# A longer lead in the gather stages of a two-layer decoder step: picks two rounds and values four rounds behind the spread

## The reference

```python
def peer(h, w_q, sub_k1, sub_k2, u_tab, v_tab):
    ...
        v1, i1 = lax.top_k(s1, P_TOPK)
        v2, i2 = lax.top_k(s2, P_TOPK)
        ...
        eid = jnp.take_along_axis(cid, j, axis=-1)
        g = jax.nn.softmax(sc.astype(F32), axis=-1)
        act = jax.nn.gelu(jnp.einsum('td,thkd->thk', xc, u_tab[eid]).astype(F32))
        return jnp.einsum('thk,thkd->td', g * act, v_tab[eid].astype(F32)).astype(h.dtype)
```

## Time and profile before

| | |
|---|---|
| runs | 2349.54, 2355.18, 2357.84 us, median 2355.18 |
| span of the profiled execution | 2353.7 us, first to last instruction |
| PE | 2044.5 us busy, 87% of the span |
| PEld | 1496.2 us, 64% |
| DVE | 1177.2 us, 50% |
| POOL | 1001.2 us, 43% |
| ACT | 650.0 us, 28% |
| gathers (software DMA queue) | 310.68 MB, 36.3% of what 16 DMA engines could be busy |
| mean granted clock of PE | 0.934 of 2.4 GHz |

### The profile page before, as it was taken

One profiled execution on the slowest core, in us unless ns is written; L12 is line 12 of the kernel. 1 busy time (PEld: TensorE's weight loads), 2 busy tenths in 40 slices (PEclk: granted clock), 3 DMA queues, 4 the chain that ended last, 5 costly groups with the idle time before them and its releaser, 6 DMA issues.

```text
span 2353.7 us, 38380 instructions
## 1 busy us (share of the span) xinstructions
PE 2044.5 (87%) x14289; PEld 1496.2 (64%) x14289; DVE 1177.2 (50%) x3447; ACT 650.0 (28%) x977; POOL 1001.2 (43%) x874
## 2 busy tenths in 40 slices
PE   9889999999997667889898889999999986777777
PEld 4554899999995323334356346999999973233332
DVE  2554699423333533578456834997233333333333
ACT  1332244545551001112134022454555520000000
POOL 0111469830004565656514303688500026666665
PEclk9899999999998798999997989999999998888878
DMA  6473434444447999999932334244444469999998
GB/s 233 173 279 119 144 129 159 161 162 162 168 163 264 331 355 369 362 329 335 350 122 62 90 116 152 81 161 153 162 168 164 165 217 348 360 346 357 365 357 312
DMA packets 179914, 529.91 MB, mean 225 GB/s; under 512 B 22066, under 2 KB 49234, under 8 KB 179474
## 3 DMA queue, kind: packets, MB, share of 16 engines
q0 software_dynamic: 87296, 310.68, 36.3%
q1 hardware_dynamic: 91282, 216.25, 26.8%
q10 hardware_dynamic: 1152, 0.52, 0.1%
HBM read 524.69 MB, written 2.69 MB: 224 GB/s over the span
## 4 chain that ended last, share of the span: by engine, by line
PE 68%; another core or an unknown queue 8%; DVE 8%; POOL 5%; issue 5%; DMA 3%; ACT 2%; SPq 1%; DVEq 0%; ACTq 0%; PEldq 0%
PE bank L950 10%; PE bank L952 10%; PE bank L951 10%; PE bank L769 8%; PE bank L1014 8%; PE bank L990 4%; POOL u_low L703 3%; PE bank L1032 3%; PE bank L1092 2%; DVE i_one_hot L2172 2%; DMA v_slot<-in_peer_v,v_rows 2%; POOL v_slot L712 2%; PE bank L979 1%; PE bank L1242 1%
## 5 line engine op out<-in xcount | busy, mean ns | idle before, releaser
L712 POOL DMA_INDIRECT v_slot<-in_peer_v,v_rows x417 | 394.6, 946 | 703.8 <-PE bank L952 441.1
L950 PE MATMUL bank<-h_parts,u_high 128*128 128x288 f32 x2048 | 607.0, 296 | 7.9 <-POOL u_low L703 6.2
L951 PE MATMUL bank<-h_parts,u_high 128*128 128x288 f32 x2048 | 604.4, 295 | 0.0
L952 PE MATMUL bank<-h_parts,u_low 128*128 128x288 f32 x2048 | 602.8, 294 | 0.0
L950 PEld LDWEIGHTS bank<-h_parts,u_high 128*128 128x128 f32 x2048 | 384.1, 188 | 11.6 <-POOL u_low L703 9.6
L952 PEld LDWEIGHTS bank<-h_parts,u_low 128*128 128x128 f32 x2048 | 385.8, 188 | 0.0
L951 PEld LDWEIGHTS bank<-h_parts,u_high 128*128 128x128 f32 x2048 | 384.6, 188 | 0.0
L1597 ACT CAST u_high<-u_slot 128x1024 fp32r<-128x1024 f32 x256 | 268.7, 1050 | 400.5 <-PE bank L952 249.1
L703 POOL TENSOR_TENSOR u_low<-u_slot,u_high 128x1024 fp32r<-128x1024 f32 x120 | 321.1, 2686 | 93.5 <-ACT u_high L1597 93.4
L1014 PE MATMUL bank<-v_slot,weight_columns 128*32 128x512 f32 x1412 | 274.1, 687 | 57.3 <-DMA v_slot<-in_peer_v,v_rows 34.1
L1014 PE MATMUL bank<-v_slot_of_columns,weight_columns 128*32 128x512 f32 x636 | 246.2, 687 | 69.8 <-DVE weight_columns L2179 44.0
(11 more groups left out here) (393 smaller groups left out, 2463.2 us busy)
## 6 DMA issues: line engine op xcount, KB each, us to landing
u_slot<-in_peer_ut SPq DMA_DIRECT2D x256, 512.0 KB, 3.5
w_q<-in_peer_w_q SPq DMA_DIRECT2D x8, 2048.0 KB, 14.4
region<-in_cache_a_kt SPq DMA_DIRECT2D x8, 960.0 KB, 11.8
region<-in_cache_a_v SPq DMA_DIRECT2D x8, 960.0 KB, 11.4
v_slot<-in_peer_v,v_rows POOLq DMA_INDIRECT x417
region<-in_ev_w_in SPq DMA_DIRECT2D x3, 2048.0 KB, 15.1
region<-in_pool_kv POOLq DMA_DIRECT2D x40, 128.0 KB, 5.0
ckv_t_norm<-in_pool_ckv SPq DMA_DIRECT2D x64, 64.0 KB
```

Source lines behind the costliest of these rows:

```text
L712: pool.indirect_dma_start(out=VS[l][slot], out_offset=None, in_=v_rows, in_offset=bass.IndirectOffsetOnAxis(ap=IDX[:, at:at + 1], axis=0)) ...
L950: pe.matmul(bank, uh, HR[:, 0, c, :], start=(c == 0), stop=False)
L951: pe.matmul(bank, uh, HR[:, 1, c, :], start=False, stop=False)
L952: ins = pe.matmul(bank, ul, HR[:, 0, c, :], start=False, stop=(c == KC - 1))
```

## The change

Two constants set the lead: the pick runs two rounds behind the spread, the values four. PE's round r does the spread of group r, the pick of group r-2 and the values of group r-4, over 76 rounds. DVE's iteration q does first the weights of group q-2, then the one-hot of group q. The waits and signals move from the helpers to the place of the call, and each step has its own wait in front of it. The wait of the one-hot for the pick of q-2 is gone as a line of its own, since the weights of q-2, which come before it on DVE now, wait for the same. The places of the key projections move back by one round (the first twenty) and by two (the others), the S5 doublings by two iterations, and the four single increments of `key_squares_used` become one of four on the last matmul. In the first layer DVE's norm of the next layer moves behind the loop, and the last tile's sum with it. Two strings of the slot plan are renamed.

```diff
+PICK_LAG, VALUE_LAG = 2, 4
+ROUNDS = NGR + VALUE_LAG
...
-NORM_PLACES = ([(q, third) for q in range(29, 39) for third in (0, 1)]
-               + [(q, third) for q in range(43, 72) for third in (0, 1, 2) if third < 2 or q % 3 == 1][0:60])
+NORM_PLACES = ([(q, third) for q in range(30, 40) for third in (0, 1)]
+               + [(q, third) for q in range(45, 74) for third in (0, 1, 2) if third < 2 or q % 3 == 1][0:60])
...
                     for i in range(4):
-                        pe.matmul(banks[7 if k else 5][32 * i:32 * i + 32, :], SUMW[:, m, :], KSQ[k // 2][:, i, :], start=(m == 0), stop=(m == 3),
-                                  skip_group_check=True).then_inc(sem("key_squares_used"), 1)
+                        ins = pe.matmul(banks[7 if k else 5][32 * i:32 * i + 32, :], SUMW[:, m, :], KSQ[k // 2][:, i, :], start=(m == 0), stop=(m == 3),
+                                        skip_group_check=True)
+                    ins.then_inc(sem("key_squares_used"), 4)
...
-                for q in range(NGR + 2):
-                    if q < NGR:
-                        spread_i1(q)
-                    key_norms(q, 0)
-                    if 1 <= q <= NGR:
-                        pick(q - 1)
-                    key_norms(q, 1)
-                    if l == 0 and q == NGR + 1:
+                for r in range(ROUNDS):
+                    if r < NGR:
+                        if r >= 2:
+
+                            pe.wait_ge(sem("one_hot_ready"), NGR * l + r - 1)
+                        spread_i1(r).then_inc(sem("i1_spread"), 1)
+                    key_norms(r, 0)
+                    if PICK_LAG <= r < NGR + PICK_LAG:
+                        pe.wait_ge(sem("one_hot_ready"), NGR * l + r - PICK_LAG + 1)
+                        if r >= PICK_LAG + 2:
+
+                            pe.wait_ge(sem("weights_ready"), NGR * l + r - PICK_LAG - 1)
+                        pick(r - PICK_LAG).then_inc(sem("picked_full"), 1)
+                    key_norms(r, 1)
+                    if l == 0 and r == ROUNDS - 1:
 
                         pe.wait_ge(sem("weights_ready"), NGR)
                         odd_norm(0)
                         odd_norm(1)
-                    if q >= 2:
-                        values(q - 2)
-                    key_norms(q, 2)
+                    if r >= VALUE_LAG:
+                        pe.wait_ge(sem("weights_ready"), NGR * l + r - VALUE_LAG + 1)
+                        values(r - VALUE_LAG).then_inc(sem("v_used"), 1)
+                    key_norms(r, 2)
...
-                for q in range(NGR + 2):
+                for q in range(NGR + PICK_LAG):
+                    if q >= PICK_LAG:
+                        weights(q - PICK_LAG)
                     if q < NGR:
+                        dve.wait_ge(sem("i1_spread"), NGR * l + q + 1)
                         one_hot(q)
-                    if 1 <= q <= NGR:
-                        weights(q - 1)
-                    if l == 0 and q == NGR + 1:
-                        odd_var(0)
-                        odd_var(1)
-                        odd_scale(0)
-                        odd_scale(1)
-                        odd_turned(0)
-                        odd_turned(1)
-                    if q - 2 in lasts:
-                        add_tile(lasts[q - 2], q - 2)
+                    if q - VALUE_LAG in lasts:
+                        dve.wait_ge(sem("v_used"), NGR * l + q - VALUE_LAG + 1)
+                        add_tile(lasts[q - VALUE_LAG])
...
-                        n = q - (first + 32)
+                        n = q - (first + 34)
...
+                if l == 0:
+                    odd_var(0)
+                    odd_var(1)
+                    odd_scale(0)
+                    odd_scale(1)
+                    odd_turned(0)
+                    odd_turned(1)
+                dve.wait_ge(sem("v_used"), NGR * (l + 1))
+                add_tile(1)
```

48 lines of the change are left out of this document (19 added, 29 removed).

## The result

The changed kernel takes 2366.39 us (median of six runs), the kernel before 2355.34 us beside it. The ratio is 1.0057, with an interval of 1.0039 to 1.0074: the change is 0.57% slower, where 0.57% faster was forecast, and the time lies outside the range. The profiled execution spans 2364.8 us, 11.1 us more than that of before.

What follows compares the result with a forecast made beforehand. Prediction: DMA engines bound the two gather stages, in the second layer held back by PE waiting for DVE's weights. 10.5 + 4.3 + 1.0 + 1.5 - 3.9 = 13.4 us off the 2353.7 span, plus 1.5 to the median: 2341.8 us, range 2330 to 2360.

Steps and rivals of the forecast that it cites:

- PE can follow: 259.90 us busy for 59 groups, 4.4 us a group: Second layer: PE needs 4.4 us a group, against 5.91 now, so PE keeps up with faster gathers.
- The stall goes to the landing of the gather: Second layer: PE's 46.3 us wait for weights goes; PE waits for gathers instead, 60 us or more, up from 21.
- The second layer, 10.5 us: Second layer's gathers: 350 us at 355 GB/s become 339.5 at 366, 10.5 us gained, bounds nothing and 27.
- The ceiling of 366 GB/s: Gather stages: rate divided by DMA share is 363 to 368 GB/s; 366 taken for an always busy DMA with gathers alone.
- The first layer, 4.3 + 1.0 + 1.5 us: Gains in the first layer's gathers: 4.3 at 980 to 1120 us, 1.0 at 1120 to 1170, 1.5 during S5 factors.
- The start, 3.9 us for both: Start of each gather stage: values of group 0 come 1.9 us later, 3.9 us lost in both layers, upper bound 12.5.
- Signals and places, 0: Moved waits, increments, key projections and S5 turns: 0 taken; projections and turns at most 2 us either way.
- at most 1 us gained: End of first layer: DVE's final work moves behind the loop, W_in1 loads wait for unchanged group 70; 0 taken.
- slower by PE's clock: Rival, second layer: granted clock falls below 0.76 and PE bounds, 2370 us; 0.10 shared with a start at its upper bound.
- The ceiling (2355): Rival, gather stages: DMA already at its ceiling, second layer gains 0 to 3 us, first 2, starts cost 3.9; chance 0.27.
- The rival for a start at its upper bound: Stage starts: two whole rounds of 3.1 us lost a layer, above 2359 us; 0.10 shared with the slower clock.
- if POOL still resumes late because the signal of a used slot is itself late, which the lead does nothing about: Sign of being wrong, gather stages: POOL's wait for used slots stays late despite the lead; no size given.

Runs made afterwards that it cites:

- free gathers: Changed kernel; values multiply rows of X, a gather into a used slot waits only for the landing before it: 2720 us, on the second kind of chip 2244.2.
- plain loads: Kernel with values on X, but SP loads rows in order in the second layer, up to eight in flight: 2241.8 us (second kind), 5.17 us a group (first).
- short start: Changed kernel; each stage's first four rounds keep lead one and two, rounds 4 and 5 carry no values: 0.9998 of before (first kind), 0.31% and 0.43% faster (second).

## Why the prediction was wrong

**What bounded the kernel.** Right: DVE's weights were what PE named, and the wait went. Wrong: that the gathers' rate is held by this wait. The step that failed is "PE can follow: 259.90 us busy for 59 groups, 4.4 us a group": it took PE's pace as its own, while on this kind of chip it is 12.9 instructions a us with three gathers in flight and 5.3 with four, and one every 1.40 us under free gathers. "The stall goes to the landing of the gather" failed with it. It went into stops of PE, 29.3 to 54.6 us, and into matmuls that take longer in the record (271 us busy for 340 us at a clock of 0.99, against 260 for 350 at 0.85). That PE falls behind under gathers is shown by the free gathers and by the plain loads on the same chip; what in the gathers, in POOL's work or in the recording does it stays open. One reading of the rows was loose too: slices 13 to 20 and 33 to 40 hold from 217 to 369 GB/s, not 345 to 370.

**The second layer, 10.5 us.** Measured: 1.2 us over 278 gathers (from +4.0 to +2.8), and nothing clear of the spread when all five traces of the first kind are taken. The ceiling of 366 GB/s from rate divided by share was wrong too, though not in a way that decided: a queue of four to nine gathers gives 409 to 410.

**The first layer, 4.3 + 1.0 + 1.5 us.** The 1.5 for the S5 factors, if anything, came: the 4.0 us of the start were made good by gather 140, and in the trace with the lead in the first layer alone they were too (+4.3 at gather 9, +0.1 at 140, against the second trace of before). Behind gather 200 it was the reverse of the forecast, +5.6 and +7.3 at the last gather. From gather 200 to the last it takes 134 to 138 us in the four traces of the first kind without the lead, 144.7 and 142.4 with it, but 136.5 with the short start, which has the long lead there as well. In 1060 to 1145 us DVE waited 10.0 us for ACT's root before its key scales, before 1.2 us, with the next one-hots and weights queued behind. That is seen, but the cause of the loss isn't shown by an experiment, and moving the places back, tried on the second kind alone, didn't help.

**The start, 3.9 us for both.** Measured 4.0 a layer in this pair of traces and 4.2 over all, so the term was sized at half. I had counted the spread and the pick at full clock and no delay. In the trace the weights of group 0 start 17.5 us after the first gather, before 16.9; PE then stands 2.81 us for the one-hot, and the spread and pick behind it take 2.35 us to the values, not 1.27, the pick alone 2.02 us where it took 1.11. The short start shows the term: it takes 4.2 us off the first ten gathers of each layer and brings the kernel level with before.

**Signals and places, 0.** The loads of the next layer's weights, w_latent first among them, were put at "at most 1 us gained" since the group they wait for is unchanged. It is, but that group was late: the load came 7.1 us later and its landing is on the path, in a gap between the stages that grew by 3.9 us, about 2 of them this wait. The new order on DVE, which I gave no price at all, is part of a rest that costs 0.22% without the lead.

**The rivals.** Nearest in time was "slower by PE's clock" (2370), and by luck: the clock rose to 0.99. The ceiling (2355) was 11 us off and was wrong as a mechanism. The Trainium skill, "DMA: Bandwidth & Descriptors", section "Where 436 GB/s comes from", has about 358 GB/s on the HBM side for a core; the kernel ran at 358 on the first kind, but free gathers ran at 409 to 410 on both kinds and plain loads at 409 on the first, so the agreement says nothing about what bounds the gathers. The rival for a start at its upper bound, 6.2 us a layer, was half right. The sentence that was right is in the last part: "if POOL still resumes late because the signal of a used slot is itself late, which the lead does nothing about". It stood there as a doubt and had no chance of its own.

## What to carry to other kernels

A wait that an engine names can be the cover of another limit: before giving its time back, look at whether the engine's pace stays the same when more transfers are in flight, by counting its instructions per microsecond against that depth. A longer lead is paid for at every start of a stage, in full, where the first slots hang on the first results; start with the short lead and let it grow. Test a change to a pipeline with the two extremes, one side free and the other side gone, and on more than one chip. Count the records of the profile as well: a stretch in which they go missing is one whose times need a second look.

## What the hardware showed that was not expected

On the first kind of chip indirect gathers at 410 GB/s bring PE to one instruction every 1.40 us, matmul or weight load, at a granted clock of 0.50, while plain loads at 409 GB/s leave it at 5.4 matmuls a us. Chips of the second kind, the same program and the same rate, show nothing of it, and the kernel before is 80 us (3.4%) faster there. In the kernel itself the stops come in pieces of 0.70 us, and PE's pace falls from 12.9 to 5.3 instructions a us between three and four gathers in flight. The profile's landing events get lost in just these stretches, down to 18% kept with free gathers, so the recording may have a part in it. What in the chips differs isn't known from these runs.
